# Four slots in the layers' closing stages, and an attention start in another order

## What is computed

```python
out = concat([oa * silu(ga), ob * silu(gb)]) @ w_out      # layer 1: (o * silu(g)) @ w_out
x = x + gt * rms(out) * g_post
# ob: y of both directions, normed by head, * gn_w + gn_b, plus sum(r * kmod * rk) * v
```

## Time and profile before

| | |
|---|---|
| three executions | 2861.0, 2861.19, 2869.78 us; median 2861.19 |
| the profiled execution | 2890.62 us, span of the core 2888.8 us |
| mean granted clock of PE in it | 0.871 of full speed |
| PE busy | 2221.3 us (77%) |
| DVE, ACT, POOL busy | 1297.9, 820.1, 694.0 us |
| DMA | 282.33 MB, mean 98 GB/s |

### The profile page before, as it was taken

How to read it: one execution, slowest core, us unless ns; L and a number is a source line. 1 busy time by engine, 2 the same in 40 slices (tenths; PEclk the granted TensorE clock), 3 DMA queues, 4 the chain that set the end, 5 groups by cost and what they waited for, 6 DMA issues and landing times. The chain is left out here.

```text
span 2888.8 us, 59301 instructions
## 1 busy us (share of the span) xinstructions
PE 2221.3 (77%) x25966; PEld 1858.1 (64%) x25966; DVE 1297.9 (45%) x1679; ACT 820.1 (28%) x1389; POOL 694.0 (24%) x616
## 2 busy tenths in 40 slices
PE   7589999922336888788589994658399968999978
PEld 1168888811126777777488884546387757888866
DVE  0344455257943544454344344545554513444422
ACT  0121133133523434444133332111333301233311
POOL 0132255111122323323210001123355624000002
PEclk9789999965668999999799886779699985899989
DMA  7622234135243222221411003232443444111143
GB/s 248 208 97 87 95 90 113 64 127 198 91 153 91 79 75 62 79 74 27 113 52 37 23 26 128 90 120 91 151 140 90 119 105 114 44 52 52 41 152 109
DMA packets 223199, 282.33 MB, mean 98 GB/s; under 512 B 59160, under 2 KB 157592, under 8 KB 221912
## 3 DMA queue, kind: packets, MB, share of 16 engines
q1 hardware_dynamic: 196432, 194.31, 22.1%
q0 software_dynamic: 20176, 81.54, 8.5%
q10 hardware_dynamic: 6336, 2.70, 0.3%
HBM read 190.54 MB, written 87.95 MB: 96 GB/s over the span
## 5 line engine op out<-in xcount | busy, mean ns | idle before, releaser
L236 PE MATMUL in_acc<-in_hi,in_whi 128*128 128x512 f32 (+1 forms) x1024 | 391.8, 383 | 20.4 <-DVE in_lo L599 16.8
L236 PE MATMUL in_acc<-in_lo,in_whi 128*128 128x512 f32 (+1 forms) x1024 | 376.0, 367 | 0.0
L236 PE MATMUL in_acc<-in_hi,in_wlo 128*128 128x512 f32 (+1 forms) x1024 | 375.8, 367 | 0.0
L236 PEld LDWEIGHTS in_acc<-in_hi,in_whi 128*128 128x128 f32 x1024 | 196.3, 192 | 59.1 <-issue 27.9
L236 PEld LDWEIGHTS in_acc<-in_lo,in_whi 128*128 128x128 f32 x1024 | 196.4, 192 | 36.9 <-issue 7.2
L236 PEld LDWEIGHTS in_acc<-in_hi,in_wlo 128*128 128x128 f32 x1024 | 195.9, 191 | 31.6
L1727 DVE TENSOR_REDUCE dense_top<-dense_score 128x1 f32<-128x640 f32 (+1 forms) x144 | 112.3, 780 | 190.0 <-PE dense_score L1814 190.0
L1727 DVE TENSOR_REDUCE window_top<-window_score 128x1 f32<-128x640 f32 (+1 forms) x128 | 101.3, 791 | 211.2 <-PE window_score L1810 211.2
L1849 PEld LDWEIGHTS dense_outs<-dense_V,dense_p 128*128 128x128 f32 x1344 | 183.5, 203 | 4.9 <-ACT dense_p L1695 0.4
L1849 PE MATMUL dense_outs<-dense_V,dense_p 128*128 128x65 f32 x1344 | 179.8, 280 | 0.0
L1849 PEld LDWEIGHTS window_outs<-window_V,window_p 128*128 128x128 f32 x1216 | 167.2, 208 | 5.0 <-ACT window_p L1695 0.6
(11 more groups left out here) (250 smaller groups left out, 5010.8 us busy)
## 6 DMA issues: line engine op xcount, KB each, us to landing
modulation_w<-in_w_mod SPq DMA_DIRECT2D x12, 2048.0 KB, 8.0
streams<-decay_out POOLq DMA_DIRECT2D x8, 2560.0 KB, 7.8
scan_L<-streams SPq DMA_DIRECT2D x80, 256.0 KB, 3.7
in_raw<-in_w_in_even SPq DMA_DIRECT2D x28, 512.0 KB, 3.8
in_raw<-in_w_in_odd SPq DMA_DIRECT2D x20, 512.0 KB, 3.8
close_ga<-gates SPq DMA_DIRECT2D x18, 512.0 KB, 4.1
gates<-in_outs POOLq DMA_DIRECT2D x32, 256.0 KB, 2.3
window_Q<-qst SPq DMA_DIRECT2D x32, 256.0 KB, 3.0
```

What stands on the lines that cost most here:

```text
L236: last = pe.matmul(out, a(k), b(k), start=(k == 0 and x == 0), stop=(k == n - 1 and x == 2))
```

## The change

In `closing`: `o`, `y`, `v` and `bo` get four slots (`NL`), the gate keeps three (`NG`) and a load of its own. A load waits for the transposes of the tile four back; a gate load for `low` three back. `gp` and `gt` get a semaphore of their own (`gains_in`), waited for only where DVE uses them, and the constants that all wait for are four in layer 0 and one in layer 1. PE runs `bonus_sums(i+3)` between `turn(i+1)` and `product(i, 1)`. In `attention`: masks and sinks are loaded before K; POOL rounds its tables first and fills KL and V after, with a semaphore `filled` for which PE waits before the turned scores and before V; the first block of output weights is loaded after the first unit is done.

```diff
@@ attention, SP
                 sp.dma_start(ident[:], ...).then_inc(loaded, 16)
                 sp.dma_start(ones[:], ...).then_inc(loaded, 16)
+                if window:
+                    sp.dma_start(masks_raw[:], edge.rearrange("a p n -> p a n")).then_inc(loaded, 16)
+                    sp.dma_start(sinks[:], ...).then_inc(loaded, 16)
...
                 load_group(0)
-                if window:
-                    sp.dma_start(masks_raw[:], edge.rearrange("a p n -> p a n")).then_inc(loaded, 16)
-                    sp.dma_start(sinks[:], ...).then_inc(loaded, 16)
@@ attention, POOL
-                pool.memset(KL[HD:P]..., 0.0).then_inc(rounded, 1)
-                pool.wait_ge(rounded, 1)
-                pool.memset(KL[HD:HD + 1]..., 1.0).then_inc(rounded, 1)
-                pool.wait_ge(rounded, 2)
                 pool.wait_ge(loaded, 16 * NCONST)
                 pool.tensor_copy(ones_r[:], ones[:]).then_inc(rounded, 1)
+                pool.wait_ge(rounded, 1)
                 if window:
-                    pool.wait_ge(rounded, 3)
                     pool.tensor_copy(eye[:], ident[:]).then_inc(rounded, 1)
-                    pool.wait_ge(rounded, 4)
+                    pool.wait_ge(rounded, 2)
                     pool.tensor_copy(masks[:], masks_raw[:]).then_inc(rounded, 1)
-                pool.wait_ge(rounded, 5 if window else 3)
-                pool.memset(V[:, :, :, HD:HW], 1.0).then_inc(rounded, 1)
+                    pool.wait_ge(rounded, 3)
+                pool.memset(KL[HD:P]..., 0.0).then_inc(filled, 1)
+                pool.wait_ge(filled, 1)
+                pool.memset(KL[HD:HD + 1]..., 1.0).then_inc(filled, 1)
+                pool.wait_ge(filled, 2)
+                pool.memset(V[:, :, :, HD:HW], 1.0).then_inc(filled, 1)
+                pool.wait_ge(filled, 3)
                 for b in range(D // BLK if prepare else 0):
+                    if b == 0:
+                        pool.wait_ge(out_done, 1)
                     if b >= 1:
                         pool.wait_ge(w_low, b)
@@ attention, PE
-                pe.wait_ge(rounded, 6 if window else 4)
+                pe.wait_ge(rounded, 3 if window else 1)
...
                     if k == 0:
+                        pe.wait_ge(filled, 2)
                         pe.wait_ge(kl_in[g], 16)
...
                     if k == 0:
+                        pe.wait_ge(filled, 3)
                         pe.wait_ge(v_in[g], 16)
@@ closing
-    NL = 3
+    NL, NG = 4, 3
...
-        ga = st.sb("ga", [P, NL, KC, P])
+        ga = st.sb("ga", [P, NG, KC, P])
...
-        NCONST = 4
+        NCONST = 1
         if rwkv:
-            NCONST = 7
+            NCONST = 4
@@ closing, SP
                 def load(i):
                     t, s = tiles[i], i % NL
                     if i >= NL:
-                        sp.wait_ge(low, i - NL + 1)
-                    sp.dma_start(ga[:, s], ...).then_inc(ga_in[s], 16)
+                        sp.wait_ge(turned, i - NL + 1)
...
+                def load_gate(i):
+                    t, s = tiles[i], i % NG
+                    if i >= NG:
+                        sp.wait_ge(low, i - NG + 1)
+                    sp.dma_start(ga[:, s], ...).then_inc(ga_in[s], 16)
...
                 sp.dma_start(ident[:], ...).then_inc(loaded, 16)
                 if rwkv:
                     sp.dma_start(sel[:]..., ...).then_inc(loaded, 16)
+                load(0)
+                if rwkv:
                     sp.dma_start(gw[:], ...).then_inc(loaded, 16)
                     sp.dma_start(gb[:], ...).then_inc(loaded, 16)
-                load(0)
-                sp.dma_start(gp[:], ...).then_inc(loaded, 16)
+                load_gate(0)
+                load(1)
+                load_gate(1)
+                sp.dma_start(gp[:], ...).then_inc(gains_in, 16)
                 for r in range(2):
-                    sp.dma_start(gt[:, r], ...).then_inc(loaded, 16)
-                for i in range(1, NL):
+                    sp.dma_start(gt[:, r], ...).then_inc(gains_in, 16)
+                for i in range(2, NL):
                     load(i)
+                load_gate(2)
                 for i in range(2):
                     load_x(i)
                 for i in range(N):
                     if i + NL < N:
                         load(i + NL)
+                    if i + NG < N:
+                        load_gate(i + NG)
                     if 2 <= i:
                         load_x(i)
@@ closing, DVE
                     if i == 0:
-                        dve.wait_ge(loaded, 16 * NCONST)
+                        dve.wait_ge(gains_in, 48)
@@ closing, PE
                 for i in range(-4, N):
-                    if rwkv and 0 <= i + 3 < N:
-                        bonus_sums(i + 3)
                     if i >= 0:
                         product(i, 0)
                     if 0 <= i + 1 < N:
                         turn(i + 1)
+                    if rwkv and 0 <= i + 3 < N:
+                        bonus_sums(i + 3)
                     if i >= 0:
                         product(i, 1)
```

More of the change, by code:

```diff
@@ L1609, in attention @@
         outs = [st.ps(f"outs{b}", [P, R * HW]) for b in range(2)]
-        (loaded, rounded, sinked, scored, topped, negated, ntopped, shifted, sink_d, sink_e, spread, lowered,
+        (loaded, rounded, filled, sinked, scored, topped, negated, ntopped, shifted, sink_d, sink_e, spread, lowered,
          turned_in, expd, pv_done, denned, inverted, out_done) = st.sems(
-            "loaded", "rounded", "sinked", "scored", "topped", "negated", "ntopped", "shifted", "sink_d",
+            "loaded", "rounded", "filled", "sinked", "scored", "topped", "negated", "ntopped", "shifted", "sink_d",
             "sink_e", "spread", "lowered", "turned_in", "expd", "pv_done", "denned", "inverted", "out_done")
@@ L1624, in _ @@
                 sp.dma_start(ones[:], consts[0:1, C_ALL:C_ALL + P].to_broadcast([P, P])).then_inc(loaded, 16)
+                if window:
+                    sp.dma_start(masks_raw[:], edge.rearrange("a p n -> p a n")).then_inc(loaded, 16)
+                    sp.dma_start(sinks[:], sink.rearrange("(a n) -> a n", a=1).to_broadcast([P, ngroups * R])
+                                 ).then_inc(loaded, 16)
                 def load(i):
@@ L1640, in _ @@
                 load_group(0)
-                if window:
-                    sp.dma_start(masks_raw[:], edge.rearrange("a p n -> p a n")).then_inc(loaded, 16)
-                    sp.dma_start(sinks[:], sink.rearrange("(a n) -> a n", a=1).to_broadcast([P, ngroups * R])
-                                 ).then_inc(loaded, 16)
                 for i in range(2, min(4, UN)):
@@ L1896, in closing @@
             "scaled", "added")
-        ga_in, o_in = (st.sems(*(f"{n}{s}" for s in range(NL))) for n in ("ga_in", "o_in"))
+        gains_in = st.sem("gains_in")
+        ga_in = st.sems(*(f"ga_in{s}" for s in range(NG)))
+        o_in = st.sems(*(f"o_in{s}" for s in range(NL)))
         x_in, stored = (st.sems(f"{n}0", f"{n}1") for n in ("x_in", "stored"))
-        NCONST = 4
+        NCONST = 1
         if rwkv:
             ydir, vtok, bonus, gn_w, gn_b = rwkv
-            NCONST = 7
+            NCONST = 4
             sel = st.sb("sel", [P, PAIRS, 8])
@@ L2073, in multiply @@
                 def multiply(i):
-                    s = i % NL
+                    s = i % NG
                     dve.wait_ge(turned, i + 1)
-                    dve.wait_ge(ga_in[s], (i // NL + 1) * 16)
+                    dve.wait_ge(ga_in[s], (i // NG + 1) * 16)
                     dve.tensor_tensor(ga[:, s], tr[:], ga[:, s], ALU.mult).then_inc(multiplied, 1)
@@ L2082, in keep_low @@
                         dve.wait_ge(summed, i - 1)
-                    dve.tensor_tensor(lo[:, i % 2], ga[:, i % NL], hi[:, i % 2].bitcast(F32), ALU.subtract).then_inc(low, 1)
+                    dve.tensor_tensor(lo[:, i % 2], ga[:, i % NG], hi[:, i % 2].bitcast(F32), ALU.subtract).then_inc(low, 1)
                 def scale(i):
```

16 lines of the change are left out of this document (8 added, 8 removed).

## The result

| | before | changed |
|---|---|---|
| executions timed together, us | 2861.0, 2861.19, 2869.78, 2871.87 | 2753.6, 2756.53, 2800.37, 2809.51 |
| median | 2865.49 | 2778.45 |
| profiled execution, its span | 2890.62, 2888.8 | 2800.37, 2798.6 |
| mean granted clock of PE in it | 0.871 | 0.878 |

The median is 87.0 us lower, 3.0%. The ratios and intervals in this document leave out executions counted as slow, those over 1.5% above a kernel's fastest: here 0.9611, 95% interval 0.9581 to 0.9641. A fifth execution of the changed kernel, not in the four, took 2753.12 us. The median lies in the range, 22 us above the forecast; two executions lie on the forecast and two about 50 us above it, and none between. The profile is of one of the latter two.

The account below looks back on a forecast made before the run. In the first closing PE was held by the bonus tile's transfer, making each tile a serial ring of 26.0 us. Gains 14.1 + 73.3 + 7.3 + 5.0 + 5.5 = 105.2 off median 2861.19 gave 2756.0 us, range 2738 to 2785.

Parts of the forecast that it names:

- First closing, start: Start of the first closing: fewer transfers gate the first work, 2.0 MB less; 5.3 us gained, ends 3 and 6.5.
- Tile 0 and the six tiles: First closing: product 0 starts at `low(0)`, 14.1 us gained with the start; six steady tiles take 82.8 us, gaining 73.3.
- PE's term of 13.8: First closing, per tile: PE's own work, two half products 11.3, transposes 0.8 and bonus sums 1.7 us, taken as the pace.
- the three limits: First closing, per tile: PE's work 13.8 us, DVE's work 13.4 to 13.5, the ring 13.5; PE's taken as highest.
- the ring: First closing, per tile: product start to transposes end 6.6 us, gate multiply to `low` end 6.9, together 13.5.
- the slow start: First closing: matmuls after idleness run at the lower clock, 1.7 us per tile; assumed saved, else 15.5 us per tile.
- Starts of window and second closing: Window attention's first matmul comes 7.3 us earlier; second closing's transposes 5.5 us earlier, through a smaller gate of transfers.
- The weight blocks: Both attentions: output-weight blocks moved after the first unit change which DVE operations POOL holds; dense gains net 5.0 us, window 0.
- net of cover: Attentions: cost of turns falling into the moved blocks, one hit of 4.2 us and half a chance of another, counted −2.9.
- for window, where one such hit precedes the wait of 3.41 us, I take 0: Window attention: the moved weight blocks were taken to bring no net gain or loss, 0 us.
- ±4.2: Attentions: 4.2 us gained for the second block's hit going, 4.2 us lost for a turn falling into a moved block.
- A longer half-rate stretch: Rival, window attention: the earlier start makes a stretch at half PE clock usual, adding 28 us, 2784 in all; chance 0.11.

Follow-up runs that it names:

- run 6: Changed kernel with PE's old order in the closing, bonus_sums before the first half product, four slots kept; one execution, 2769.17 us, first closing 182.5.
- run 7: Changed kernel with three slots instead of four, loads waiting for the transposes three tiles back, new order kept; one execution, 2753.84 us, first closing 180.7.
- run 8: Changed kernel with three slots and loads waiting for `low` as before, PE's new order kept; one execution, 2773.26 us, first closing 187.3.
- run 12: Kernel before the change with only bonus_sums moved behind turn; one execution, 2795.74 us, against 2859.42 for the kernel before; first closing 197.9.
- run 2: Changed attention with the closing of before; median 2852.44 us of 12 executions, ratio 0.9947 to the kernel before.
- run 10: The changed kernel again, nothing edited; median 2765.11 us of six, ratio 0.9651 to the kernel before.
- run 3: Changed kernel without the first weight block's wait for the first unit; median 2773.56 us, ratio 0.9668 to the kernel before.
- run 11: Changed kernel with three slots in the closing and each `w_lo` waiting for a unit's turn on DVE; median 2736.69 us, ratio 0.9574 to the kernel before.
- run 9: Changed kernel with each POOL `w_lo` waiting for a given unit's turn on DVE; median 2742.29 us, ratio 0.9579 to the kernel before.
- run 1: Changed closing with the attention of before; median 2778.58 us, ratio 0.9668 to the kernel before.

## Why the prediction was right, and where it wasn't

**First closing, start: right.** Forecast 5.3 us from 2.0 MB less at the rate of the earlier trace rows, measured 4.6. The other kernels with this gate begin at 10.1 to 11.1 us, so up to 5.8.

**Tile 0 and the six tiles: right.** Product 0 is 37.9 us after the stage's start, before 51.3: 13.5, forecast 14.1. Six tiles take 82.2 us instead of 156.1: 73.9, forecast 73.3. PE's term of 13.8 was 0.7 too high by the bonus sums: 1.7 us in the earlier trace rows, taken at the lower clock, 0.96 us in the rows above. With that corrected, PE's sum is 13.1, and the highest of the three limits is not PE's, as the working had it. It is the third one, the ring: forecast 6.6 + 6.9 = 13.5, measured 6.76 + 6.94 = 13.70. The three limits lay so close that the number didn't depend on the choice. The clock is at 1.00 from 44 us into the stage to 177, and the six tiles lie in it, so the slow start was not kept. The Trainium skill, "TensorE: Matmul & The Clock Gate", Part 1, has the low rate as the default that activity lifts; for the closing the trace agrees (50 us of half rate, 136 before), for the window stage it doesn't explain 71 us at 0.50 with PE busy in 68.5 of them.

**Credit went to the wrong part.** The working counted four slots, moved gate and moved step as one. Runs 6, 7, 8 and 12 part them. The moved step alone brings 71 us; with loads in the new order of `closing`, but still three slots and the wait for `low`, 81.9; with the wait for the transposes and three slots, all of it; and four slots with that wait bring all of it without the moved step. What paid was that the ring of the earlier trace rows was opened, and more than one edit does that.

**Starts of window and second closing: right.** Window 9.5 us after the stage's start, forecast 9.6; second closing 5.6 us gained in the transposes, forecast 5.5.

**The weight blocks: the sign in dense right, the price wrong.** "A unit's turn falls into one of them perhaps once" was about right. The Trainium skill, "GPSIMD Engine Reference", Specifications, has it that POOL shares its SBUF interfaces with DVE and contends with DVE instructions that have two SBUF inputs or run in a two-port mode. The traces agree for `ntop` and `sd` of the window stage, which have two inputs: the hold of 3.56 us ended with the POOL operation. The agreement of 4.8 with 5.0 us in dense is luck, by the spread of that stage above, and the −2.9 "net of cover" in the sum isn't worked out from any row. The failed step is "for window, where one such hit precedes the wait of 3.41 us, I take 0", and the ±4.2 by which every hit was priced. A hit costs not its hold. It costs the half-rate stretch behind it, units that take 19.6 us instead of 10.9. Over the profiles, from run 2 (361.6 us, 31 at half rate) to run 10 (416.6, 144), a microsecond at half rate makes the window stage 0.49 longer; 137 instead of 31 is then some 52 us, against the 48.6 by which the two lengths 410.2 and 361.6 differ. Not all of it is the hit's: some 34 us of the 106 lie in the lead-in, where the clock rose at 63 us and not at 29, and 71 behind the held turn. The stretches behind the ten falls in window stages last 10 to 71 us, so a hit cost an estimated 5 to 35 us, where the sum had at most 4.2. What sets their length stays open.

**The rival that came true in half of the executions.** "A longer half-rate stretch" had a chance of 0.11 and the sentence "Nothing in the profile ties it to what is changed". That sentence is wrong. The earlier trace rows showed the tie, an empty PE of 3.41 us just ahead of the slow stretch, and the trace of before shows what stood in front of it:

```profile
2431.00:2436.00 5.00, 3.33 (x24) 2.94 (x23) 4.93 (x4) 0.00 (x0) 4.92 (x2) 1.00 0.00 0
2436.00:2441.00 5.00, 3.26 (x12) 2.97 (x13) 2.36 (x5) 1.88 (x4) 0.93 (x1) 0.66 0.26 76
...
2432.47 4.49 DVE L1751 TENSOR_TENSOR window_sd<-window_ntop,window_sinks_up 128x4 f32<-128x4 f32 x1
```

A `w_lo` was under way (POOL busy 4.92 of 5 us), the last operation of a turn took 4.49 us, and the clock went from 1.00 to 0.66 and then down, within 10 us. The forecast, 2756.0, fits the two executions with the higher clock, which were not profiled. The other two lie 44 and 54 us above it, where the rival had 28: it was sized by one stretch of some three and a half units (about 65 us), and these executions have 100 to 123 us more at half rate than the short ones. That the median of four came out at 2778.45 is in part a draw: it is the middle of a gap between 2756.53 and 2800.37, and six executions in run 10 gave 2765.11. The prediction's own measure of noise, 0.3%, came from three executions; seventeen of the kernel before spread over 2.2%.

**Which holds are followed by a fall.** Listed as DVE operation held → PE empty behind it, us, for holds that met a clock at 1.00. Window stages, clock stayed: 2.70 → 1.40, 1.74 → 1.08, 2.09 → 0.97, 1.80 → 0.92, 1.85 → 0.92, 1.85 → 0.78. Clock fell: 2.97 → 1.94, 2.13 → 2.32, 3.56 → 2.52, 4.05 → 2.71, 4.11 → 2.75, 1.73 and 1.22 in one turn → 2.77, 4.49 → 3.13, 4.29 → 3.26, 4.49 → 3.41, 2.27 and 4.46 in one turn → 4.62. The length of the hold doesn't sort them (2.70 stayed, 2.13 fell): it matters how much of it reaches PE. These are all ten falls in a window stage after its lead-in, each behind a held turn, and the window stages without a held turn in the steady part (runs 2, 3, 7 and 11), or with PE empty for under 1 us behind it (run 9), had none. Dense is less clear. The clock stayed behind 1.22 → 1.87, 1.90 → 1.50 and 2.36 → 1.43; it fell, for 3 to 13 us only, behind 2.62 → 2.23, 2.71 → 2.31 (twice), 4.27 → 3.87, and 1.54 and 4.88 in one turn → 5.33. Four more holds (4.89 → 3.93, 4.89 → 3.77, 4.46 → 3.79, 3.22 → 2.54) stand 59 to 66 us into the stage, where seven other profiles have a fall with no hold, so they show nothing. And in the closing of run 12 an empty PE of 1.05 us was followed by 3.4 us at half rate. So the list sorts the window stages and is no limit for others.

**What stays open.** When the clock first rises in the window stage differs between 29 and 70 us after its start, and in runs 8 and 10 it fell again in that lead-in with no hold ahead. In run 12 it fell there behind one of 1.69 us, with PE empty for 0.98. In the four profiles whose blocks start with the stage (before and runs 1, 3, 12) it is up for good only at 70 us, in the ten others at 29 to 63; whether the blocks' loads or holds do that was not tried by itself. Dense has four places (62, about 148, 232 and 300 us into the stage) where it drops, mostly for 7 to 28 us, at the context's narrow matmuls, with PE empty for only 0.5 us. These are in before and after alike. Whether the change makes holds likelier than before isn't shown: seventeen executions of before spread over 63 us, four of the changed kernel over 56, and one profile is one throw.

## What to carry to other kernels

Where one engine's in-order program waits for a transfer, look at what stands behind the waiting instruction: moving it behind the work that is ready is one edit, and here it was worth 71 us of 86. Price a wait of TensorE in a dense matmul stream by the clock that follows and not by its own length, and look for what GpSimd was doing when VectorE was late. A large GpSimd operation in a stage with small, urgent VectorE steps belongs behind such a step by a semaphore; here the medians of six differ by 23 us for it (0.8%), and by 28 with three slots besides. Cutting it into pieces that follow each other showed no gain.

## What the chip did that was not expected

- A DVE operation of 128x4 elements, 0.16 us alone, took up to 4.49 us beside a POOL subtraction of 128x2048 (4.54 us), until that ended; it hit operations with two inputs (`ntop`, `sd`) and, in dense, some with a single input (`top`, 3860 ns in the earlier trace rows). Reductions from PSUM were not held in any profile. POOL's cast held them for up to 1.85 us.
- After a fall in a window stage PE stayed at half rate for 10 to 71 us, in part of it with 5.00 of 5 us busy, before the clock was granted again, in before as well as in the changed kernel (the rows at 2350 and 2400 above). What PE did before was to stand empty, for 1.94 to 4.62 us in these ten cases.
- Executions of one kernel, with the same data, differ by 2% (2841.85 to 2905.17 before, 2753.6 to 2809.51 changed). Most of the difference is time at half rate: in the seventeen, span times granted clock spreads over 19 us, the time over 63.
